# Two packed steps of the inverse on each side of half a burst of key scores, in three of four head pairs

## What is computed

```
proj = x @ w_in_l
q, k, v, beta, g = dn_prep(short_conv(x_pad, conv_w), ba, aa, a_log, dt_bias)
L = where(tri_strict, einsum('bhncd,bhned->bhnce', kbeta, k) * decay, 0)
sol = triangular_solve(L, rhs, lower=True, unit_diagonal=True)   # (I + L)^-1 rhs
gate = einsum('bqhd,bhnd->bqhn', qf, kmean)                      # samples: keys from a paged pool
```

## Time and profile before

| | before |
|---|---|
| median of three runs | 1550.68 us |
| lowest, highest | 1548.36, 1551.88 us |
| profiled execution | 1550.67 us |
| its span, first to last instruction | 1548.9 us |
| TensorE busy, share of the span | 1504.1 us, 97% |
| VectorE busy | 913.6 us, 59% |
| ScalarE busy | 647.6 us, 42% |
| DMA, mean over the span | 236 GB/s |

### The profile page before, as it was taken

The page is one execution under the profiler, slowest core; times in us unless marked ns, Lnnn a source line. Parts: engine busy times, 40 slices in busy tenths (PEclk is TensorE's granted clock), DMA queues, the critical chain, the costliest instruction groups (busy, mean ns, idle before and its releaser), DMA issues.

```text
span 1548.9 us, 36648 instructions
## 1 busy us (share of the span) xinstructions
PE 1504.1 (97%) x15464; PEld 1456.2 (94%) x15464; DVE 913.6 (59%) x1217; ACT 647.6 (42%) x769; POOL 90.7 (6%) x126
## 2 busy tenths in 40 slices
PE   7999999999999999999999999999999999999996
PEld 7999898989889999987999999999999999999995
DVE  4444646468743467763886666666666544445566
ACT  5444343434425444554544344543333332333434
POOL 0000000002244001001000000000000000000000
PEclk9999999999999999999999999999999999999998
DMA  8799779795678967547545454556766655555453
GB/s 305 275 370 346 291 296 362 281 390 207 253 280 322 348 243 260 201 166 264 196 164 181 172 187 166 190 177 216 270 230 245 217 181 174 188 178 176 163 181 117
DMA packets 72528, 365.11 MB, mean 236 GB/s; under 512 B 9073, under 2 KB 10426, under 8 KB 45658
## 3 DMA queue, kind: packets, MB, share of 16 engines
q1 hardware_dynamic: 56962, 310.00, 55.9%
q0 software_dynamic: 13664, 52.31, 9.1%
q10 hardware_dynamic: 1792, 1.20, 0.3%
HBM read 353.20 MB, written 10.47 MB: 235 GB/s over the span
## 4 chain that ended last, share of the span: by engine, by line
PE 87%; DVE 5%; ACT 3%; issue 2%; DMA 2%; SPq 1%; ACTq 0%; DVEq 0%
PE psum_g L556 24%; PE psum_g L557 24%; PE psum_g L558 24%; PE M L2252 4%; DVE wl L540 2%; PE M L2408 1%; PE M L556 1%; PE M L557 1%; PE M L558 1%; ACT wh L535 1%; PE psum_g L2614 1%; PE M L2267 1%; PE M L2277 1%; DMA pj<-x_t 1%; DMA raw<-w_out_t 0%
## 5 line engine op out<-in xcount | busy, mean ns | idle before, releaser
L556 PE MATMUL psum_g<-xh,wh 128*128 128x264 f32 (+1 forms) x2382 | 694.1, 291 | 5.5 <-issue 2.2
L558 PE MATMUL psum_g<-xh,wl 128*128 128x264 f32 (+1 forms) x2382 | 676.8, 284 | 1.7 <-issue 1.7
L557 PE MATMUL psum_g<-xl,wh 128*128 128x264 f32 (+1 forms) x2382 | 677.4, 284 | 0.0
L540 DVE TENSOR_TENSOR wl<-raw,wh 128x2048 fp32r<-128x2048 f32 (+1 forms) x205 | 461.6, 2252 | 287.1 <-ACT wh L535 286.5
L535 ACT CAST wh<-raw 128x2048 fp32r<-128x2048 f32 (+1 forms) x221 | 414.6, 1876 | 240.5 <-PE psum_g L558 201.7
L556 PEld LDWEIGHTS psum_g<-xh,wh 128*128 128x128 f32 x2382 | 450.2, 189 | 16.9 <-issue 12.3
L557 PEld LDWEIGHTS psum_g<-xl,wh 128*128 128x128 f32 x2382 | 450.6, 189 | 5.4 <-issue 5.2
L558 PEld LDWEIGHTS psum_g<-xh,wl 128*128 128x128 f32 x2382 | 448.8, 188 | 0.0
L556 PE MATMUL psum_g<-gh,wh 128*128 128x264 f32 x704 | 200.4, 285 | 0.2 <-DVE wl L540 0.2
L558 PE MATMUL psum_g<-gh,wl 128*128 128x264 f32 x704 | 199.4, 283 | 0.0
L557 PE MATMUL psum_g<-gl,wh 128*128 128x264 f32 x704 | 199.4, 283 | 0.0
(11 more groups left out here) (474 smaller groups left out, 1694.9 us busy)
## 6 DMA issues: line engine op xcount, KB each, us to landing
raw<-w_t SPq DMA_DIRECT2D x88, 1024.0 KB
raw<-w_in_t SPq DMA_DIRECT2D x53, 1024.0 KB
kring<-cache_k_t SPq DMA_DIRECT2D x96, 512.0 KB, 6.2
sraw<-cache_k_t SPq DMA_DIRECT2D x32, 512.0 KB, 7.0
raw<-w_out_t SPq DMA_DIRECT2D x16, 1024.0 KB
raw<-w2a_t SPq DMA_DIRECT2D x16, 1024.0 KB
raw<-w2b_t SPq DMA_DIRECT2D x16, 1024.0 KB
raw<-w2c_t SPq DMA_DIRECT2D x16, 768.0 KB
```

What stands on the lines that cost most here:

```text
L540: eng.tensor_tensor(wl[:, u % 2, 0:nk], raw[:, u % 2, 0:nk], wh[:, u % 2, 0:nk].bitcast(F32), ALU.subtract).then_inc(raw_used, 1)
L556: nc.tensor.matmul(out, hi_w, x_hi(k), start=(k == order[0]), stop=False)
L557: nc.tensor.matmul(out, hi_w, x_lo(k), start=False, stop=False)
L558: last = nc.tensor.matmul(out, lo_w, x_hi(k), start=False, stop=(k == order[-1]))
```

## The change

In pairs 0 to 2 the twelve inverse steps go two at a time in six places instead of three at a time in four: steps 7 and 8 behind unit r = 1; 9 and 10 behind the eighth k-tile of r = 2; 11 and 12 behind r = 2; 13 and 14 behind the eighth k-tile of r = 3; 15 and 16 behind r = 3; 17 and 18 behind the eighth k-tile of r = 4. In the units r = 2, 3, 4 the first half of the burst moves to the eighth k-tile too, between the two steps there. Pair 3 is as before. ScalarE, GpSimd and SyncE have the same program.

```diff
             if p < 3:
-                return tuple(range(3 * r + 4, 3 * r + 7)) if place == 3 else ()
+                first = {(1, 3): 7, (2, 1): 9, (2, 3): 11, (3, 1): 13, (3, 3): 15, (4, 1): 17}.get((r, place))
+                return (first, first + 1) if first else ()
...
                     if first:
                         delta(p, first)
+                    if first and p < 3:
+                        for burst in bursts_at(u):
+                            score(burst // 4, burst % 4, range(0, 4))
...
+                halved = p < 3 and tiles_at(u, 1)
                 for j in bursts_at(u):
-                    for half in range(2):
+                    for half in (1,) if halved else (0, 1):
                         score(j // 4, j % 4, range(4 * half, 4 * half + 4))
```

## The result

Before and after on the same chips: 1550.38 us (median of 20 executions, 1546.86 to 1553.43) and **1552.82 us** (20 executions, 1550.08 to 1556.58), a ratio of 1.0022 with a 95% interval of 1.0015 to 1.0029. The ratio compares the two samples as a whole; by it the change costs 2.3 to 4.5 us, by the medians 2.4. The forecast was 1552.9 in a range of 1548.0 to 1557.0. The 0.2% that I had set as the bound of "no change" lies inside the interval, so which side of it the result is on is not decided; that it is slower at all is. The profiled execution of after took 1554.39 us, its span 1552.6.

What follows compares the result with a forecast made beforehand. TensorE's instruction order, busy for 97% of the span, was taken as the bound. Terms -5.3 + 1.8 + 2.0 + 3.7 = +2.2 us on 1550.67 gave 1552.9 us, range 1548.0 to 1557.0.

Steps and rivals of the forecast that it cites:

- Block borders: TensorE's holes stand at borders of 256-instruction blocks, whose fetch starts only once the block before is entered; borders placed by count.
- The rival by which the holes have another cause: Block crossings are mostly hidden, so moving instructions need not remove holes: gain nothing, result 1556.2; no separate chance given.
- What stays: Behind unit 12 the hole of 2.2 us and its slow clock stay whole, since r = 1 keeps its order.
- What is removed: Holes behind units 20, 22 and 29 shrink or go, with one slow stretch: 5.3 us gross, 0.4 left of the first.
- New holes: Blocks holding packed steps in the new order: late ones overrun by 0.2 to 0.7, 2.0 us in all, between 0 and 5.3.
- a mean need of 4.3 us: Average time from entering a block until TensorE could leave it, over four late blocks; set against new spans of 5.1 to 7.
- my four: The late blocks entered at 164.4, 249.8, 272.1 and 343.1, which could be left 4.7, 5.9, 2.9 and 3.9 us later.
- The wait on VectorE: At r = 3, step 16 waits for VectorE's step 15, behind the convolution: 1.2 us in three pairs, 3.7 us; none at r = 2.
- The breaks: Three more places per pair where a unit is broken open, 0.20 us each, nine of them: 1.8 us added on TensorE.
- Pages and raw loads: The first half burst wants pages 5 to 6 us sooner and a raw load goes some 4 us later: no cost.
- The sum: -5.3 removed, + 1.8 breaks, + 2.0 block waits, + 3.7 VectorE wait = +2.2 us, giving 1552.9 us.
- the 1.3 us of slow clock: Matmuls behind unit 20's hole, 255.66 to 258.48, ran at the lower clock level; full clock expected there, 1.3 us gained.

Runs made afterwards that it cites:

- e4: The kernel before with ten tiny 32x32 products (40 instructions) added in unit 11, so later borders fall 40 instructions earlier: 1559.75 us, ratio 1.0077.
- e2: The changed kernel with the first half burst of r = 1 also moved to the eighth k-tile: 1551.1 us, ratio 1.0012 to before.
- e7: The kernel before, loading only the first quarter of each page of keys from the third burst on: 1539.99 us, a single execution.
- e1: The changed kernel with VectorE's convolution put ahead of step 13 at r = 3 of pairs 0 to 2: 1548.8 us, ratio 1.0001 to before.
- e3: The changed kernel with both edits, those of e1 and e2: 1547.01 us, ratio 0.9985 to before.
- e5: The kernel of e4 with 216 more instructions (54 tiny products) in unit 32, putting later borders back in place: 1559.05 us, ratio 1.0062 to before.
- e6: The same kernel as e4, repeated on another chip: 1558.31 us, ratio 1.0058 to before.

## Why the prediction was right, point by point

**Block borders.** Right, and it carries the prediction: every border in after stands at the instruction that the count gave, and e4 moved each hole with 40 instructions and nothing else. The rival by which the holes have another cause is out. So, here, is the rule of the Trainium skill ("Runtime: NRT & Kernel Launch", section "Instruction fetch mechanics") that crossing a block is mostly hidden: it doesn't hold where 256 instructions last about 3 us. Nor is it only those: over all these runs, from 100 to 560 us, the holes at borders stand behind blocks whose own work takes 2.6 to 5.7 us, most such blocks under 4 us have one and some of those of 5 us; behind longer blocks there is none. One wording is too strong: that a fetch starts "only once the one before is entered". Counted by TensorE's own starts, some packets go up to 1.8 us ahead of that (at 378.15 for a block entered at 379.9, in before); the look-ahead is of one block all the same.

**What stays.** The hole behind unit 12 was said to stay whole: 1.82 us idle in before and 1.80 in after, slow clock after it in both (0.83 granted from 165 to 175 us). The row of before:

```profile
169.09 0.41 PE L2252 MATMUL M<-kring,pj 128*32 128x128 f32 x3 [1.82 <-issue]
```

e2 takes it down to 0.45 with half a burst moved, a little over the 0.3 at most that was expected.

**What is removed.** 2.4 + 1.3 + 0.4 + 1.2 as forecast, with 0.47 (0.4 forecast) left of the first and full clock behind it.

**New holes: the term that was too small.** 0.47 + 1.25 + 0.3 + 0.8 = 2.8 us, for 2.0. The blocks that run late overran by up to 1.25, where I had said 0.2 to 0.7. I worked with a mean need of 4.3 us. The block entered at 257.35 could be left only at 263.58, 6.2 us later, beyond even the longest of my four (5.9); its packet started 3.85 us after the entry. What a single block needs depends on what is in flight when it is fetched (e7). A mean is the wrong figure for a sum in which only the late blocks count.

**The wait on VectorE.** 1.2 us three times, 3.7 in all, on step 15's operation ahead of step 16: place, count and size as worked out from the chain of six durations in the earlier trace rows. e1 took away the wait, with a new hole of 0.8 in its place, and gave 2.7 us back by the starts and 3.3 by the ratios. r = 2 has no such wait, as forecast.

**The breaks.** 1.8 us was assumed from the earlier trace rows. In pair 0 no hole changes, so its +1.9 less the wait of 1.23 leaves 0.7 for three breaks, 0.2 each. One of them, ahead of step 13, in after: from 184.08 to 184.29.

```profile
184.08 0.28 PE L559 MATMUL psum_g<-xh,wl 128*128 128x264 f32 x1
184.29 0.45 PE L2278 MATMUL M<-chain 32*32 32x32 f32 x32
184.67 1.08 PE L2253 MATMUL M<-kring,pj 128*32 128x128 f32 x32
185.69 0.45 PE L2278 MATMUL M<-chain 32*32 32x32 f32 x32
```

**Pages and raw loads.** No cost, as forecast: 0.4 for 0.3 us of waiting on pages. The cover is thin, though: with a half burst moved at r = 1 too (e2, e3) it went, and TensorE stood 0.4 to 0.65 us for pages.

**The sum.** With the measured terms it is -5.3 + 1.8 + 2.8 + 3.7 = +3.0, and the changed stretch shows +3.6 (after starts it 0.4 us ahead of before and leaves it 3.2 behind); 0.6 is not assigned. Over the program the two profiled executions differ by 3.7, the medians by 2.4. That these come out near +2.2 is in part luck: the 1.3 us of slow clock that I counted as gained were gained at 255 us, but slow stretches of the same kind stand at about 170, 255 and 733 us in before and at about 170, 436 and 515 in after, three and three, so that over the program the clock gave nothing back. The windows 434 to 441 us of before and of after, the clock being the third number from the end:

```profile
434.00:441.00 7.00, 5.75 (x150) 4.67 (x148) 4.33 (x18) 3.54 (x8) 1.15 (x2) 1.00 0.83 330
```

```profile
434.00:441.00 7.00, 5.05 (x68) 4.68 (x71) 1.83 (x10) 0.55 (x3) 2.91 (x3) 0.76 0.84 298
```

In after TensorE stood for 2.16 us at 435.95 just ahead of it, in before for 1.74 at 432.69 with no drop. Both holes stand at the same instruction, 9 x 256 instructions (to within two) behind the hole of unit 29, so this is a border too, with 2.16 us in one profiled execution and 1.74 in the other. What shifts the slow stretches I didn't test; they make the +3.2 at 367 us rise to +5.2 at 618 and fall to +3.7 at the end.

## What to carry to other kernels

Where a stretch of small products makes an in-order engine issue 256 instructions in under some 5 to 6 us while the DMA engines are full, count the instructions from border to border: the holes stand where the blocks end, and half a burst moved can take one away or put one in. Before steps are moved earlier, write out the order of every engine that takes part in them; here VectorE's fixed order turned a gain into a loss of 3.7 us, and moving an independent operation into its idle time ahead of the step gave some 3 us back. Compare two orders of such a kernel only with the borders in mind, for 40 instructions alone moved this one by 0.6 to 0.8%.

## What the runs showed that I had not expected

- A border can cost 3.1 us (e4, inside step 12), more than any of before: the fetch of its block started 3.6 us after the block before was entered, with the DMA share at 1.05 from 174 to 177 us.
- The same border can be free in one kernel and cost 0.79 us in another (274.8 in after, 274.99 in e1), with the fetch started 2.4 and 4.0 us after the entry.
- Fifty-four 32x32 products that all write the same place took 3.5 us, 65 ns each, where 1.3 in all was expected (e5); the counterweight of an experiment needs a price of its own.
- Emptier DMA engines don't remove every hole: at a share of 0.52 one of over 1.1 us was left, beside a single large load (e7).
- After holes of 1.8 to 2.3 us in which TensorE stood, the granted clock fell to its lower level for 3.4 us in some places (behind units 12 and 20, at 435.95 in after: 0.76 over 7 us) and not in others (1.74 us at 432.69 in before). The length of the hole alone doesn't order them: e6 has the lower level behind a hole of 1.60 us at 256.64 (0.72 from 256 to 262 us). What decides was not settled.
